# Moving the norm of one attention output tile behind four softmax units of the next head group

## The reference, cut to what matters

```python
def rms_norm(x, gain=None):
    y = xf * lax.rsqrt(jnp.mean(xf * xf, axis=-1, keepdims=True) + NORM_EPS)
    ...
    attn = p[:, :, 0] - lam * p[:, :, 1]
    return jnp.einsum('bhqk,bkhe->bqhe', attn.astype(v.dtype), v)
...
o = rms_norm(o, subln_g) * (1.0 - lam_init)      # o: 256 tokens x 4 heads x 128; 1 - lam_init = 0.8
...
return jnp.concatenate([o_a, o_b], axis=-1) @ w_out
```

## Time and profile before

| what | us |
|---|---|
| median of 3 runs | 1329.2 (1328.51 to 1332.69) |
| the profiled execution, its own time | 1330.42 |
| its span, first to last instruction | 1328.6 |
| PE busy | 1237.5 (93%) |
| DVE busy | 374.9 (28%) |
| ACT busy | 221.7 (17%) |
| POOL busy | 116.9 (9%) |

### The profile page before, as it was taken

One profiled execution on the slowest core, in us unless ns is written; L12 is line 12 of the kernel. 1 busy time (PEld: TensorE's weight loads), 2 busy tenths in 40 slices (PEclk: granted clock), 3 DMA queues, 4 the chain that ended last, 5 costly groups with the idle time before them and its releaser, 6 DMA issues.

```text
span 1328.6 us, 18945 instructions
## 1 busy us (share of the span) xinstructions
PE 1237.5 (93%) x8035; PEld 708.6 (53%) x8035; DVE 374.9 (28%) x924; ACT 221.7 (17%) x499; POOL 116.9 (9%) x147
## 2 busy tenths in 40 slices
PE   6999999999999999988988999999999999989898
PEld 3444467655555455544545456765555555545454
DVE  3574864301021010111014884330101101111012
ACT  2223432401111110101110024230101010010001
POOL 2002000320030130030000010010000000000000
PEclk9999999999999999999998999999999999999999
DMA  9994876899999999999999873779999999999995
GB/s 367 407 347 127 319 321 247 343 427 428 427 426 429 427 427 428 427 427 429 427 424 408 310 267 139 297 314 427 427 427 427 428 427 427 427 427 428 428 426 225
DMA packets 54137, 502.13 MB, mean 378 GB/s; under 512 B 4944, under 2 KB 6232, under 8 KB 23200
## 3 DMA queue, kind: packets, MB, share of 16 engines
q1 hardware_dynamic: 50160, 493.05, 89.1%
q0 software_dynamic: 2304, 5.11, 1.3%
q10 hardware_dynamic: 1584, 2.69, 0.5%
HBM read 493.47 MB, written 7.36 MB: 377 GB/s over the span
## 4 chain that ended last, share of the span: by engine, by line
PE 61%; DMA 29%; DVE 6%; ACT 1%; issue 1%; SPq 0%; DVEq 0%; ACTq 0%; PEldq 0%
DMA ring<-in_moe_w 22%; PE B L891 22%; PE B L909 11%; PE A L919 5%; DMA both<-in_moe_w 5%; PE A L806 4%; PE B L710 4%; PE B L723 2%; PE B L653 2%; DMA ring<-in_ada_w 2%; PE B L617 2%; PE B L606 1%; DVE work L1545 1%; PE B L1159 1%; DVE work L1231 1%
## 5 line engine op out<-in xcount | busy, mean ns | idle before, releaser
L891 PE MATMUL B<-ring,work 128*64 128x256 f32 x2592 | 306.7, 390 | 13.3 <-DMA ring<-in_moe_w 13.2
L891 PEld LDWEIGHTS B<-ring,work 128*64 128x64 f32 x2592 | 182.0, 134 | 127.8 <-issue 15.7
L909 PE MATMUL B<-ring,work 128*64 128x512 f32 x880 | 199.2, 595 | 10.7 <-DMA ring<-in_moe_w 9.9
L1539 DVE TENSOR_TENSOR work<-work,B 128x256 f32<-128x256 f32 x64 | 39.5, 617 | 581.0 <-PE B L891 581.0
L919 PE MATMUL A<-work 128*128 128x256 f32 x512 | 118.2, 384 | 16.0 <-DVE work L1545 16.0
L909 PEld LDWEIGHTS B<-ring,work 128*64 128x64 f32 x880 | 61.3, 136 | 117.0 <-issue 95.2
L919 PEld LDWEIGHTS A<-work 128*128 128x128 f32 x512 | 94.9, 190 | 35.3 <-issue 23.9
L1961 ACT COPY work<-B 64x512 f32<-64x512 f32 x64 | 37.2, 581 | 458.0 <-PE B L909 458.0
L1545 DVE COPY work<-B 64x512 f32<-64x512 f32 x64 | 43.7, 683 | 199.3 <-PE B L909 199.3
L2233 POOL COPY work<-work 128x512 f32 x60 | 36.9, 615 | 697.7 <-PE B L891 655.3
L1953 ACT ACTIVATE work<-B 128x256 f32<-128x256 f32 x64 | 24.5, 383 | 324.8 <-PE B L891 324.8
(11 more groups left out here) (304 smaller groups left out, 1070.8 us busy)
## 6 DMA issues: line engine op xcount, KB each, us to landing
ring<-in_moe_w SPq DMA_DIRECT2D x136, 2048.0 KB, 32.2
work<-in_moe_w SPq DMA_DIRECT2D x25, 2048.0 KB, 32.9
ring<-in_ada_w SPq DMA_DIRECT2D x24, 2048.0 KB, 19.8
both<-in_moe_w SPq DMA_DIRECT2D x21, 2048.0 KB, 33.3
early<-in_moe_w SPq DMA_DIRECT2D x10, 2048.0 KB, 31.7
ring<-in_ev_w_in SPq DMA_DIRECT2D x6, 2048.0 KB, 18.8
ring<-in_od_w_in SPq DMA_DIRECT2D x4, 2048.0 KB, 15.8
ring<-in_ev_w_out SPq DMA_DIRECT2D x2, 2048.0 KB, 16.7
```

The costliest lines, as they stand in the source:

```text
L891: ins = pe.matmul((B5, B6)[m][64 * h:64 * h + 64, FH * m:FH * m + FH], xs[:, k, :], w[:, k, :].rearrange("p (q h j) -> p h q j", h=2, j=2) ...
L909: ins = pe.matmul(B7[64 * m:64 * m + 64, :], hidTb[:, k % 2, k // 2, :], w[:, k, 512 * m:512 * m + 512], start=(k == 0), stop=(k == KF - 1))
L1539: dve.tensor_tensor(hid[:, :].rearrange("p (j q) -> p q j", j=2), silu_a[:, 0:FH].rearrange("p (q j) -> p q j", j=2), B6[:, FH:FF].rearran ...
```

## The change

`out_rows_a` is cut in two. `copy_rows_a` holds the wait and the copy; `norm_rows_a` the rest, with its squares written to `tmp16` where they went to `sc_sb[:, 1 - t]`, since `sc_sb` is the score buffer of the running units. Tile 0 runs both parts one after the other, where it was. For tile 1 DVE runs the copy where it was and the norm after B unit 3. ACT's `root(8)` moves to the hook of step 4 of its group B loop: after the exponentials of unit 3 and the copy of the transposes of unit 2, before the exponentials of unit 4.

```diff
-            def out_rows_a(t, pv):
+            def copy_rows_a(t, pv):
                 dve.wait_ge(pv_done, pv)
                 o = htok[:, t, 0:512].rearrange("p (h d) -> p h d", h=4)
                 dve.tensor_copy(o, B5[:, :].rearrange("p (h d) -> p h d", h=4)).then_inc(oa_copied, 1)
+
+            def norm_rows_a(t):
+                o = htok[:, t, 0:512].rearrange("p (h d) -> p h d", h=4)
                 dve.wait_ge(oa_copied, t + 1)
-                sq = sc_sb[:, 1 - t].rearrange("p a b -> p (a b)").rearrange("p (h d) -> p h d", h=4)
+                sq = tmp16.rearrange("p a b c -> p (a b c)").rearrange("p (h d) -> p h d", h=4)
                 tt(sq, o, o, ALU.mult)
...
                 if j == 3 + LAG_PV:
-                    out_rows_a(0, 4)
+                    copy_rows_a(0, 4)
+                    norm_rows_a(0)
             set_norm(1, 12, 1536)
-            out_rows_a(1, 8)
+            copy_rows_a(1, 8)
             for j in range(NA):
                 softmax_unit(NA, j, *B_UNITS[j], sc_sb, prob_b)
+                if j == 3:
+                    norm_rows_a(1)
...
             qk_evac("B", 8, 1)
-            root(8, small[:, 0:4])
             ada_evac(0, "c2")
 
             def beside_b(j):
 
+                if j == 4:
+                    root(8, small[:, 0:4])
                 if j == 5:
```

## The result

The changed kernel takes 1334.2 us (median of 20 executions, 1331.7 to 1338.9) against 1331.2 of the kernel before (20 executions, 1328.5 to 1335.1). The ratio is 1.0024, 95% interval [1.0015, 1.0033]: slower by some 3.2 us, 2.0 to 4.4. Forecast were +0.8 us and 1330.0, in a range to 1332.5. The sign holds and the change stays within 0.3%, but the size was too small and the time lies outside the range. The kernel before had 1329.2 in the three executions that the prediction had, 2.0 less than in twenty. One execution of the kernel before, in a later run, took 2410.7 us at a mean clock of 0.893, where all others on record have 0.988 or more; it is left out of that run's ratio.

A forecast was written before the change was run, and what follows sets the result against it. Bound: the experts' DMA stream, which waits for the packed rows, so mixer time counts one for one. Terms -2.5 - 1.2 + 3.7 - 0.3 + 1.1 = +0.8 us, from median 1329.2 to 1330.0; range 1327.0 to 1332.5.

The forecast's parts named there:

- The front: Group B's start, before unit 0: without tile 1's norm DVE starts 2.5 us earlier; ACT's table load stays hidden.
- ACT's order holds the root, unit 4 comes late: Middle of group B: root waits behind unit 2's transpose copy and a table load; unit 4 starts 1.0 us late.
- Rival A: Norm after unit 3: root taken when DVE asks, norm lies in idle time; -4.0 us, 1325.2; chance 0.10.
- The hole: PE between oA0 and oA1: waits some 3.3 us for the bank that ACT's copy of unit 3 frees.
- The low clock behind it: PE from about 180, after its 3.3 us wait: clock of 0.50 expected, costing 1.1 us (bounds 0 and 1.5).
- Rival B: PE after its 3.3 us wait before oA1: no low clock follows; -0.3 us, 1328.9; chance 0.17.
- The drain at the table load: ACT's root: a drain of about 1.38 us per table switch makes its path 1.4 longer, sum +2.2; chance 0.03.
- The low clock of the kernel before as a fixed price: PE at 169 to 172.4: half clock after thin work costs 1.5 us; its removal was credited with 1.2.
- the low clock in both places: PE at 169 and again after its 3.3 us wait before oA1: +2.3 us, 1331.5; chance 0.15.
- One execution's time carried to the median: Whole kernel: profiled execution 1330.42 lies 1.2 above the median 1329.2; +0.8 from that median gives 1330.0.
- The clock elsewhere, put at nothing: PE beyond the mixer stretch around the moved norm: the sum has no term for a changed clock there.

## Why the prediction was wrong in size and right in kind

- *The front.* Right: 2.50 us less ahead of unit 0, the low clock at 169 gone, the table load hidden.
- *ACT's order holds the root, unit 4 comes late.* Right: the reciprocal was forecast 13.5 us after the copy and came at 13.2; unit 4 at 15.8, came at 15.5. Root one place earlier: hole 1.44; root out: 0.83. Rival A, that the gain stays, is out for this order; in the stretch the norm in two parts comes near it (3.7 us shorter than in the profile before, 4.0 by A).
- *The hole.* 3.3 forecast, 3.31 measured. `oA1`, behind it, starts some 0.4 us earlier after the copy than before; forecast was 0.3.
- *The low clock behind it.* Forecast 1.1 us; it is 1.6, since none of it falls into the hole: the low clock began 1.5 us after the hole's end. This is the mis-sized term of the sum for the stretch: +0.8 forecast, +1.1 measured against the profile that was read. Rival B (no low clock) is out, five of five.
- *The drain at the table load.* Out: 0.02 us between load and root.
- *The low clock of the kernel before as a fixed price.* This step failed. I credited the change in full with taking away 1.2 us of the 1.5, from one profile. The old low clock comes in three of four profiles, the new one in five of five. From 26.3 against 25.1 (three times) and 23.6 (once), the mean local loss is 26.3 - 24.7 = 1.6 us. I had given 0.18 to the low clock in both places or the drain, on the thought that the old stretch stays; none of the changed kernel's profiles has it.
- *One execution's time carried to the median.* The forecast of 1330.0 went out from 1329.2, the median of three; it was 1331.2 with twenty. That alone is 2.0 us of the 4.2 by which it missed, and the spread of 4 us within those three had been on the table.
- *The clock elsewhere, put at nothing.* This step failed too, and it is the larger part of what the sum lacks. The sum has no term for PE's clock outside the stretch. 1.6 of some 3.3 us of loss are shown in the stretch; the rest, 1.7 with an uncertainty of 1, goes with lower mean clocks: 23 against 15 us at the low level, of which the stretch accounts for 1 and the place at 704 for some 4. By the timed executions this is hardly chance: 8 of the 12 of the changed kernel have a mean clock of 0.992 or less, against 9 of the 35 of the kernel before beside them. Over all runs it is 21 of 32 against 22 of 106.
- *What stays open.* Why low clocks come more often later on with a change made at 170, and where most of their price falls. At 704 the longer low stretch shows as 0.3 us of the stage on average (476.9 against 476.6 us); for mixer 1 three profiles in five against two in four show no difference. Also open is why the early root, whose stretch is 1.9 us shorter than the old order's mean of 24.7, gains nothing in time.

## What to carry to other kernels

Work moved into one engine's idle time may need a partner engine: look where the partner's instruction lands in its own order, what stands before it there, and add the function table it must load. Cut the moved piece at the point where it waits for the other engine, and put the halves behind different units; here that turned a loss of 3 us into a gain of 1.7 (0.4 to 3.1). And a low clock that one profile shows is one draw: before it is credited or charged, take several executions, or fill the stretch and measure what it costs.

## What the runs showed of the hardware that I had not expected

- The same thin work on PE (0.18 and 0.12 in two of three microseconds) was followed by 1.2 GHz in three profiles and not in a fourth. A hole of 3.3 us was followed by it in five of five profiles, a hole of 1.44 us in the one profile that has it was not.
- The low level can last while PE is shown busy all the time: 10 us at a clock of 0.50 with PE busy 10.00 of 10 us, in mixer 1.
- PE can stand 2.3 to 4.0 us within a row of products with no wait shown, in 13 of 13 profiles. Five to twenty products added 500 us or more earlier remove it, in 5 of 5 profiles of four kernels. The way from the packed rows to mixer 1 is then 2.5 us shorter, though in one of the five the packed rows came 2 us later.
- A table load is followed by its function after 0.01 to 0.02 us, with no further delay, where nothing else is waited for (173.72 + 1.28, then the root at 175.02).
